# Where a norm's factor per token enters: ahead of the mixing products, or at their evictions

## What the kernel computes

```python
h = rms_norm(x, norm1_g[i])
proj = h @ w_in[i]
q, k, v, z, xbc, dt_raw, gate_a, gate_m = jnp.split(proj, SPLITS, axis=-1)
q = rms_norm(q.reshape(b, s, ATTN_HEADS, 2, ATTN_HEAD_DIM), qk_norm_g[i, 0])
k = rms_norm(k.reshape(b, s, ATTN_HEADS, 2, ATTN_HEAD_DIM), qk_norm_g[i, 1])
...
u = jax.nn.silu(conv(xbc) + conv_b)          # five taps along the tokens, each channel by itself
y = y_f + y_b + X * d_skip[:, None]          # two scans, forward and backward, from u and dt
ym = rms_norm(y * jax.nn.silu(z), norm_g) @ w_ssm_out
merged = jax.nn.sigmoid(gate_a) * ya + jax.nn.sigmoid(gate_m) * ym
x = x + (merged @ w_out[i])
x = x + hier_moe(rms_norm(x, norm2_g[i]), ...)
```

## Time and profile before

| | us |
|---|---|
| median of three runs | 1735.32 |
| the profiled execution | 1734.33 |
| its span, from the first to the last instruction | 1732.5 |
| TensorE busy | 1686.1 |
| VectorE busy | 718.0 |
| ACT busy | 683.6 |
| GpSimd busy | 667.9 |

### The profile page before, as it was taken

The page is one execution under the profiler, slowest core; times in us unless marked ns, Lnnn a source line. Parts: engine busy times, 40 slices in busy tenths (PEclk is TensorE's granted clock), DMA queues, the critical chain, the costliest instruction groups (busy, mean ns, idle before and its releaser), DMA issues.

```text
span 1732.5 us, 23236 instructions
## 1 busy us (share of the span) xinstructions
PE 1686.1 (97%) x8975; PEld 1046.0 (60%) x8975; DVE 718.0 (41%) x1351; ACT 683.6 (39%) x1549; POOL 667.9 (39%) x536
## 2 busy tenths in 40 slices
PE   8999999999999999999899999999999999999997
PEld 6889877787434444343378898777874344444342
DVE  6728788524222222221176287875242222122121
ACT  5565787754211111111156557877541111111111
POOL 7788776895000000000077987768940000000000
PEclk9999999999999999999999999999999999999999
DMA  7454312766999999999954452227589999999997
GB/s 285 184 195 152 141 50 102 284 265 275 408 428 428 427 428 427 426 428 428 424 212 162 179 195 98 84 106 283 233 320 414 427 428 427 427 428 428 426 427 311
DMA packets 44659, 528.47 MB, mean 305 GB/s; under 512 B 4824, under 2 KB 7640, under 8 KB 12288
## 3 DMA queue, kind: packets, MB, share of 16 engines
q1 hardware_dynamic: 44512, 526.89, 74.1%
q0 software_dynamic: 32, 0.02, 0.0%
HBM read 525.82 MB, written 1.06 MB: 304 GB/s over the span
## 4 chain that ended last, share of the span: by engine, by line
PE 70%; DMA 13%; DVE 9%; ACT 5%; issue 2%; POOL 1%; SPq 0%; DVEq 0%; ACTq 0%
PE PS L1286 19%; DMA view<-in_w_exp_up_dram 12%; PE PS L1317 11%; PE PS L870 8%; PE PS L872 8%; PE PS L871 8%; DVE view L1987 5%; PE PS L1232 3%; PE PS L1218 2%; DVE view L1983 1%; PE PS L1077 1%; PE PS L1219 1%; ACT view L1555 1%; DMA wr<-in_w_router_dram 1%; PE PS L858 1%
## 5 line engine op out<-in xcount | busy, mean ns | idle before, releaser
L2368 POOL TENSOR_TENSOR view<-view,view 128x512 fp32r<-128x512 f32 x448 | 579.8, 1317 | 543.2 <-ACT view L1441 532.4
L1286 PE MATMUL PS<-view,view 128*64 128x512 f32 x2044 | 455.4, 595 | 19.2 <-DMA view<-in_w_exp_gate_dram 9.9
L1441 ACT ACTIVATE view<-view 128x512 fp32r<-128x512 f32 x448 | 274.5, 631 | 150.7 <-PE PS L872 147.7
L1286 PEld LDWEIGHTS PS<-view,view 128*64 128x64 f32 x2044 | 143.1, 137 | 301.3 <-issue 263.5
L870 PE MATMUL PS<-view,view 128*128 128x512 f32 x704 | 285.4, 405 | 5.1 <-POOL view L2368 3.2
L872 PE MATMUL PS<-view,view 128*128 128x512 f32 x704 | 275.1, 391 | 0.0
L871 PE MATMUL PS<-view,view 128*128 128x512 f32 x704 | 274.9, 391 | 0.0
L2268 DVE SCALAR_TENSOR_TENSOR view<-PS,gcol,view 128x512 fp32r<-128x512 f32 x64 | 48.0, 751 | 476.3 <-ACT view L1754 459.0
L1317 PE MATMUL PS<-view,stb 128*64 128x512 f32 x1024 | 227.7, 596 | 4.4 <-ACT stb L1730 1.5
L1317 PEld LDWEIGHTS PS<-view,stb 128*64 128x64 f32 x1024 | 70.3, 137 | 137.3 <-issue 125.6
L870 PEld LDWEIGHTS PS<-view,view 128*128 128x128 f32 x704 | 132.5, 188 | 32.6 <-issue 5.1
(11 more groups left out here) (263 smaller groups left out, 2028.1 us busy)
## 6 DMA issues: line engine op xcount, KB each, us to landing
view<-in_w_exp_up_dram SPq DMA_DIRECT2D x60, 2048.0 KB, 26.9
view<-in_w_exp_gate_dram SPq DMA_DIRECT2D x60, 2048.0 KB, 26.9
view<-in_w_mix_dram SPq DMA_DIRECT2D x54, 2048.0 KB, 7.6
view<-in_w_exp_down_dram SPq DMA_DIRECT2D x54, 2048.0 KB, 28.8
view<-in_w_exp_down_dram SPq DMA_DIRECT2D x16, 1024.0 KB, 23.9
view<-in_w_mix_dram SPq DMA_DIRECT2D x8, 512.0 KB, 17.9
view<-in_w_exp_gate_dram SPq DMA_DIRECT2D x2, 1792.0 KB, 9.4
view<-bias_table SPq DMA_DIRECT2D x2, 1536.0 KB, 11.8
```

The source lines that it names most:

```text
L1286: ins = pe.matmul(bank(ph, name, j)[e * CAP:(e + 1) * CAP, :], xgT1[:, k, at + e * CAP:at + (e + 1) * CAP], weight_rows(j, kind, row, 1), ...
L1441: nc.scalar.activation(highs(chunk), weights(slot8, chunk), ACT.Copy).then_inc(*high_ready.up(ph))
L2368: g_.tensor_tensor(weights(low8, chunk), weights(slot8, chunk), highs(chunk), ALU.subtract).then_inc(*low_ready.up(ph))
```

## The change

The transposes take x itself, so the products of the mixer are made from rows without the norm's factor. The sums of squares and the factor are still made, later:

- ACT squares the rows of x in block 0, behind the casts of the next block's first two chunks; VectorE makes the factor `r_tok` behind the eight low tiles, and with it `e_tok`, the token's mean square (with its 1e-6) times 1e-6. The head norms of q and k take `e_tok` in place of the 1e-6 (`floor`), so the variance takes two instructions, one per token tile.
- v, z and the gates get the factor as ACT's scale at their evictions, `dt` in two VectorE instructions in place of one.
- The convolution tiles lie with the channels on the partitions, so the factor is there one per column. Two matmuls (`spread`) behind block 1 spread it over a tile of 128x256, ACT copies it to `r_cols`, and VectorE multiplies each of the 24 PSUM tiles by it in place, ahead of the taps.
- GpSimd no longer waits for XN, the bridge between the layers is one filler matmul instead of seven.

```diff
         f += [(("p", b, t), (2 * b + t) % 4) for t in range(TT)]
+        if b == 1:
+            f += [(("spread",), 4)]
...
                 def row_turn(k):
-                    pe.wait_ge(*xn_ready.at(ph, 4 if k >= KD // 2 else 2))
-                    transpose2(ph, lambda t: XN[:, t, k * P:(k + 1) * P], ("hT", k))
+                    for t in range(TT):
+                        if l:
+                            pe.wait_ge(*out_of(Phase(l - 1), "s", ALL_PAIRS - 1, t, k // (KD // 2)))
+                        else:
+                            pe.wait_ge(s_x[t], 16)
+                    transpose2(ph, lambda t: X[:, t, k * P:(k + 1) * P], ("hT", k))
...
+                    if b == 1:
+                        pe.wait_ge(*row_ready.at(ph, 1))
+                        pe.wait_ge(*free(ph, "spread"))
+                        for t in range(TT):
+                            ins = pe.matmul(bank(ph, "spread")[:, t * P:(t + 1) * P], r_tok[t].to_broadcast([P, P]),
+                                            ident[:, :], start=True, stop=True)
+                        ins.then_inc(*fill(ph, "spread"))
...
-                    bridge(7)
+                    bridge(1)
...
                     cast(ph, nxt, 2)
+                    for i in range(0 if b else 2 * TT):
+                        t, n = i % 2, i // 2
...
+                        nc.scalar.activation(sq[:, i * COLS:(i + 1) * COLS], X[:, t, n * COLS:(n + 1) * COLS],
+                                             ACT.Square, accum_out=small[:, i:i + 1]).then_inc(*sumsq.up(ph))
...
                         if b < 4:
-                            if b:
-                                act.wait_ge(*rs_in.at(ph, 1 + b))
+                            act.wait_ge(*rs_in.at(ph, 1 + b))
...
-                                                 ACT.Silu).then_inc(*drain(ph, "p", b, t))
+                                                 ACT.Silu, scale=r_tok[t]).then_inc(*drain(ph, "p", b, t))
...
+                        v.tensor_scalar(var[:, 0:8], var[:, 0:8], 1.0 / width, floor[0], ALU.mult, ALU.add
+                                        ).then_inc(*dve_step.up(ph))
+                        v.tensor_scalar(var[:, 8:16], var[:, 8:16], 1.0 / width, floor[1], ALU.mult, ALU.add
+                                        ).then_inc(*rs_in.up(ph))
...
                     r = rsqrt(TT, 1, D)
-                    for n in range(2):
-                        for t in range(TT):
-                            v.tensor_scalar(XN[:, t, n * COLS:(n + 1) * COLS], X[:, t, n * COLS:(n + 1) * COLS], r[:, t:t + 1],
-                                            None, ALU.mult).then_inc(*xn_ready.up(ph))
+                    each(lambda t: v.tensor_scalar(e_tok[t], st[:, t:t + 1], EPS, None, ALU.mult))
+                    v.tensor_copy(st[:, 80:80 + TT], r).then_inc(*row_ready.up(ph))
+                    dve.wait_ge(*row_ready.made(ph))
-                norm_rows()
                 for k in range(KD):
                     low_of(hTh[:, k, :], hTl[:, k, :], ("hT", k), k + 1, vcol[:, G1 + k:G1 + k + 1])
+                norm_rows()
                 if l == 0:
                     head_scales(ph)
...
+                    link(v.tensor_tensor(x_, x_, r_cols, ALU.mult))
                     link(v.tensor_scalar(a, x_, w(2), vcol[:, CB + c:CB + c + 1], ALU.mult, ALU.add))
...
-                if l:
-                    low(0, 2)
-                pool.wait_ge(*xn_ready.at(ph, 4))
-                low(2 if l else 0, 2 * CHUNKS)
+                low(0, 2 * CHUNKS)
```

More of the change, by code:

```diff
@@ L442, in encoder @@
         small = sb("small", [P, 48])
+        r_tok, e_tok = ([st[:, o + t:o + t + 1] for t in range(TT)] for o in (80, 86))
         dtv, av, nac, eac, dend = (dtm[:, i] for i in range(5))
@@ L1466, in layer @@
                                          ).then_inc(s_tabc, 1)
-                cast(ph, 2 if l else 0, HIGHS - (2 if l else 0))
+                cast(ph, 0, HIGHS)
                 act.wait_ge(*columns_in.at(ph, 1))
@@ L1486, in layer @@
                     cast(ph, nxt, 2)
+                    for i in range(0 if b else 2 * TT):
+                        t, n = i % 2, i // 2
+                        if l:
+                            act.wait_ge(*out_of(Phase(l - 1), "s", ALL_PAIRS - 1, t, n))
+                        else:
+                            act.wait_ge(s_x[t], 16)
+                        nc.scalar.activation(sq[:, i * COLS:(i + 1) * COLS], X[:, t, n * COLS:(n + 1) * COLS],
+                                             ACT.Square, accum_out=small[:, i:i + 1]).then_inc(*sumsq.up(ph))
                     if b == 1:
@@ L1502, in layer @@
                         elif b == 4:
-                            nc.scalar.activation(V[:, t, 0:COLS], bank(ph, "p", b, t), ACT.Copy
+                            act.wait_ge(*row_ready.at(ph, 1))
+                            nc.scalar.activation(V[:, t, 0:COLS], bank(ph, "p", b, t), ACT.Copy, scale=r_tok[t]
                                                  ).then_inc(*drain(ph, "p", b, t))
@@ L1522, in layer @@
                         cast(ph, nxt + 4, 3)
+                    if b == 1:
+                        act.wait_ge(*full(ph, "spread"))
+                        nc.scalar.activation(r_cols, bank(ph, "spread")[:, 0:TT * P], ACT.Copy).then_inc(*drain(ph, "spread"))
                     if 1 <= b <= 4:
@@ L1608, in layer @@
                                 act.wait_ge(*full(ph, name, 0, t))
-                                nc.scalar.activation(dst, bank(ph, name, 0, t), ACT.Copy
+                                nc.scalar.activation(dst, bank(ph, name, 0, t), ACT.Copy, scale=r_tok[t]
                                                      ).then_inc(*drain(ph, name, 0, t))
@@ L1625, in sigmoid @@
                         act.wait_ge(*full(ph, name, 1, t))
-                        nc.scalar.activation(to[:, t, :], bank(ph, name, 1, t), ACT.Sigmoid
+                        nc.scalar.activation(to[:, t, :], bank(ph, name, 1, t), ACT.Sigmoid, scale=r_tok[t]
                                              ).then_inc(*drain(ph, name, 1, t))
@@ L1822, in link, with rsqrt @@
                     dve.wait_ge(*dve_step.made(ph))
-                def rsqrt(n, count, width, done=None):
+                def rsqrt(n, count, width, done=None, floor=None):
                     var, half, y, a, r = (st[:, o:o + n] for o in (0, 16, 32, 48, 64))
-                    v.tensor_scalar(var, var, 1.0 / width, EPS, ALU.mult, ALU.add).then_inc(*rs_in.up(ph))
+                    if floor is None:
+                        v.tensor_scalar(var, var, 1.0 / width, EPS, ALU.mult, ALU.add).then_inc(*rs_in.up(ph))
+                    else:
+                        v.tensor_scalar(var[:, 0:8], var[:, 0:8], 1.0 / width, floor[0], ALU.mult, ALU.add
+                                        ).then_inc(*dve_step.up(ph))
+                        v.tensor_scalar(var[:, 8:16], var[:, 8:16], 1.0 / width, floor[1], ALU.mult, ALU.add
+                                        ).then_inc(*rs_in.up(ph))
+                        dve.wait_ge(*dve_step.made(ph))
                     dve.wait_ge(*rs_in.made(ph))
@@ L1906, in layer @@
                                              AX, ALU.add))
-                    r = rsqrt(16, 2 + b, HD)
+                    r = rsqrt(16, 2 + b, HD, floor=e_tok)
                     for t in range(TT):
@@ L1920, in layer @@
                 dve.wait_ge(*full(ph, "dt"))
-                v.tensor_tensor(X0, PS[:, 4, 0:P].rearrange("p (t h) -> p t h", t=TT),
-                                bc_dt.unsqueeze(1).to_broadcast([P, TT, 64]), ALU.add
-                                ).then_inc(*drain(ph, "dt"))
+                for t in range(TT):
+                    ins = v.scalar_tensor_tensor(out=X0[:, t, :], in0=PS[:, 4, t * 64:(t + 1) * 64], scalar=r_tok[t],
+                                                 in1=bc_dt, op0=ALU.mult, op1=ALU.add)
+                    if t == 0:
+                        ins.then_inc(*dve_step.up(ph))
+                ins.then_inc(*drain(ph, "dt"))
+                dve.wait_ge(*dve_step.made(ph))
                 dve.wait_ge(*out_of(ph, "dt"))
@@ L1982, in layer @@
                         dve.wait_ge(*u_ready.at(ph, c - 2))
+                    if c == 0:
+                        dve.wait_ge(*out_of(ph, "spread"))
+                    link(v.tensor_tensor(x_, x_, r_cols, ALU.mult))
                     link(v.tensor_scalar(a, x_, w(2), vcol[:, CB + c:CB + c + 1], ALU.mult, ALU.add))
```

9 lines of the change are left out of this document (4 added, 5 removed).

## The result

The changed kernel takes 1759.61 us (median of four runs, 1757.32 to 1760.31) against 1735.57 of the kernel before on the same chip: a ratio of 1.0136, 95% interval [1.012, 1.0152], slower. The forecast was 1755. The profiled execution, the fastest of the four, took 1757.32 us (span 1755.6), 22.99 more than that of before.

The account below looks back on a forecast made before the run. TensorE, busy 97% of the span, was taken as the bound. First layer -0.3+9.5+2.5+1.6=+13.3 us, second -5.4+8.0+2.5+1.6=+6.7, together +20.0 on 1734.33, median 1.0 above: 1755, range 1736 to 1764.

Parts of the forecast that it names:

- the waits: Sign: TensorE waits 6 to 10 us before block 0's transposes in both layers.
- the slow norm steps: Sign: VectorE steps of 1.2 us each in the row norm.
- the products 0.43 apart: Sign: TensorE products run 0.43 us apart after its wait for block 0.
- the convolution tile: Sign: a VectorE tile in the convolution takes 3.1 us or more.
- The moved norm: Block 0: norm steps under GpSimd's subtractions delay the transposes, costing 9.5 us in the first layer, 8.0 in the second.
- TensorE after the wait: Behind block 0's wait, TensorE runs at half pace for a while, costing 2.5 us in each layer.
- The second layer's start: Transposes need only the row additions and the shorter bridge costs nothing, so the first product gains 5.4 us.
- The first layer's start: GpSimd's first subtraction moves up, so the first product waits only for the low tile; gain 0.3 us.
- The convolution: One more VectorE PSUM instruction on each of 24 tiles a layer, 0.45 to 0.58 us, costs 1.6 a layer.
- the terms put at nothing: Eviction factors, extra variance and dt instructions, and spread matmuls counted as free; uncovered about 1 us.
- Rival 3: Convolution-bound: the PSUM instruction costs 0.58 us a tile, 4.2 a layer, giving 1760.5 us; chance 0.15.
- Rivals 1, 2 and 4: Faster, norm steps at 0.2 us, 1731 to 1733, chance 0.08; half the cost, 1741, 0.20; expert stream hides delay, 1735, 0.05.

Follow-up runs that it names:

- noif: Changed kernel without TensorE's branch over the overflow pass after each layer's expert units; 1750.01 us, ratio 1.0077 to the kernel before.
- best: Changed kernel with earlier row squares, the norm's root and spread moved behind block 2's chain, and a hint ahead of TensorE's jump; 1732.78 us, 0.9981 to the kernel before.
- shield: Changed kernel with GpSimd held ahead of its third subtraction for block 1 until the row norm is done; 1746.61 us, ratio 1.0087 to the kernel before.
- hint: Changed kernel with an early likely-taken hint for TensorE's overflow jump, the branch rewritten with named targets; 1750.25 us, ratio 1.0092 to the kernel before.
- before_bridge1: Kernel before with one bridging filler matmul instead of seven, nothing else changed; 1741.11 us, ratio 1.0029 to the kernel before.
- bridge7: Changed kernel with the seven bridging matmuls of the kernel before instead of one; 1754.67 us, ratio 1.0099 to the kernel before.
- before_hint: Kernel before with one bridging matmul instead of seven and the hint ahead of TensorE's jump; 1735.74 us, ratio 1.0002 to the kernel before.

## Why the prediction was right, and where it was not

The direction and the place were right, the time 4.6 us short. Of its signs the waits, the slow norm steps and the products 0.43 apart came; the convolution tile came at the edge, 3.09 us for 3.1 or more; a first product 5.4 us sooner in the second layer did not come. By its steps:

- **The moved norm.** Shown: waits of 7.08 and 6.14 us, norm steps of 1.2 us under GpSimd and of 0.16 where GpSimd is held. First layer 8.1 for 9.5; second 9.5 for 8.0, of which noif puts 32.46 - 30.68 = 1.8 on the half pace of the late start, so 7.7 for 8.0. The steps fell otherwise than laid out: six of the norm's instructions, two variances and two of the chain's were put under GpSimd for the second layer; the trace has five of the norm's, no variance and five of the chain's.
- **TensorE after the wait.** 1.46 and 2.14 for 2.5; the granted clock reads 0.50 from 44 to 48 us and from 916 to 922, and 0.99 and 1.00 behind. It comes with the wait: "best", which waits 0.67, has 12.03 and 12.01, and shield pays it in block 1, where its wait is. The half pace lasts about 3.4 and 5.6 us here, and 3 to 6 us behind such waits in the other kernels.
- **The second layer's start: the step that failed.** "The shorter bridge ends with the transposes and costs nothing" was wrong, and with it the gain of 5.4: 0.37 came. The data were there when the step said so, as noif and hint show with 5.48. What was missed is the jump: I priced the bridge by its matmuls and not by what they covered. It cost 5.1 us, and about 1.8 more for the slow pace behind.
- **The first layer's start.** 0.83 for 0.3: the casts began at 9.05 instead of 9.53 us, which the prediction held fixed.
- **The convolution.** The nearest row was right (0.43 us for 417 ns), the lag of the first tiles too large: 1.05 and 0.98 for 1.6 a layer. Of the first layer's 1.05, 0.68 lies between the first tile and the attention (81.13 us before, 81.81 after); the other 0.37 comes ahead of the first tile, among the terms put at nothing. Rival 3 asked for 0.58 us a tile and 4.2 a layer; its time, 1760.5, is nearer the result than the forecast's, for a reason that did not occur.
- **Rivals 1, 2 and 4.** TensorE's waits exclude 1 and 2. The delay of the first layer was not made up in the expert stream beyond 1.02 us, within its scatter: 4 is out.

The sum of the forecast, 20.0, came near 22.99 because a missed 5.0 + 1.8 was partly paid by terms sized too high: 1.4 + 0.3 of the norm, 1.4 of the pace, 1.2 of the convolution, 0.5 of the first start; 1.0 of scatter comes on top. That the total lies so near is in part luck.

What stays open: why the second gap of before_bridge1 lies between the first and the second transpose, whether the hint alone or the form of its branch removes the wait, why shield's runs spread over 12 us, and what part of the 7 us each single slow step carries; "best" shows only that moving the norm's start and its tail together removes it.

## What to carry to other kernels

Before a filler or a wait is shortened, list everything between it and the next useful instruction on that engine's own program, jumps included: here an idle stretch without a releaser was the engine's own stream. A hint well ahead of a branch that is nearly always taken was worth 5.1 us here. A short chain of tiny VectorE steps on SBUF beside GpSimd costs by where GpSimd's pauses lie, so move its producer earlier and its tail later together; either alone handed the collision to the next chain here.

## What the runs showed of the hardware that I had not expected

- A taken jump on TensorE left it idle for 4.40 to 4.73 us (before_bridge1, changed; up to 5.08 in shield), with one 0.02 MB packet of q8 about 3 us ahead of the next instruction. Six more matmuls of 0.9 us ahead of the jump hide the idle time wholly (bridge7), and so does the branch with a hint (hint, before_hint).
- After TensorE waits of 2.1 to 7.1 us products run at half pace (0.43 us apart, the granted clock at 0.50) for 3 to 6 us, in shield only from 1.1 and 1.3 us after the wait on; after waits of up to 0.7 us inside a block they keep their pace (changed at 28.75, "best"). Yet the earlier trace rows show half pace at the program's start under a granted clock of 1.00.
